# One decoder step of a 64-expert model on one core: the expert loop in 48 pairs of blocks instead of 96 single ones

## The reference

```python
scores = sigmoid(t @ w_r)                       # 264 x 64
idx = top 8 of 64, from the 4 best of 8 groups  # by scores + bias
gates = chosen scores / their sum * 2.5
for e in range(64):                             # 64 experts, 1024 -> 256 -> 1024
    a = silu(t @ wg[e]) * (t @ wu[e])
    routed += gates[:, e] * (a @ wd[e])
out = routed + shared expert
```

## Time and profile before

| what | value |
|---|---|
| runs, median (lowest to highest) | 1795.79 us (1793.62 to 1798.0) |
| the profiled execution | 1778.79 us, span 1777.1 us, granted clock 0.957 |
| PE busy | 1629.6 us, 92% |
| DVE busy | 957.6 us, 54% |
| POOL busy | 697.3 us, 39% |
| moved by DMA | 588.84 MB, mean 331 GB/s |

### The profile page before, as it was taken

How to read it: one execution, slowest core, us unless ns; L and a number is a source line. 1 busy time by engine, 2 the same in 40 slices (tenths; PEclk the granted TensorE clock), 3 DMA queues, 4 the chain that set the end, 5 groups by cost and what they waited for, 6 DMA issues and landing times.

```text
span 1777.1 us, 27285 instructions
## 1 busy us (share of the span) xinstructions
PE 1629.6 (92%) x10621; PEld 914.1 (51%) x10621; DVE 957.6 (54%) x2368; ACT 238.9 (13%) x607; POOL 697.3 (39%) x755
## 2 busy tenths in 40 slices
PE   7898999999899999999779989999998999899984
PEld 4674775444445444444367557644444444444433
DVE  3887468544345544444379754764443444354436
ACT  3223331000002100000031343100000000000001
POOL 1306007554445554444102240365554455355420
PEclk9998999999999999999979979999999999999996
DMA  9668467999999999999965866599999999999955
GB/s 326 226 237 289 154 266 277 400 364 357 401 408 400 385 413 393 377 382 360 346 239 190 287 216 235 189 395 412 410 389 409 346 387 405 367 386 399 413 209 207
DMA packets 185918, 588.84 MB, mean 331 GB/s; under 512 B 67705, under 2 KB 85837, under 8 KB 131902
## 3 DMA queue, kind: packets, MB, share of 16 engines
q1 hardware_dynamic: 115504, 506.99, 73.1%
q0 software_dynamic: 67232, 79.73, 13.0%
q10 hardware_dynamic: 3054, 0.38, 0.2%
HBM read 775.22 MB, written 56.95 MB: 468 GB/s over the span
## 4 chain that ended last, share of the span: by engine, by line
PE 80%; DVE 8%; DMA 5%; issue 3%; ACT 1%; ACTq 1%; SPq 0%; POOL 0%; DVEq 0%; POOLq 0%
PE ps L1420 39%; PE ps L1433 18%; PE ps L1122 4%; PE ps L953 4%; PE ps L1268 3%; DMA raw<-in_exp_w_up,idx_w 3%; PE ps L1009 2%; PE ps L1380 1%; DMA ypart<-yrows_k 1%; DVE ysum L2277 1%; PE ps L986 1%; PE ps L1017 1%; ACTq L577 1%; PE ps L1200 1%; PE ps L1253 1%
## 5 line engine op out<-in xcount | busy, mean ns | idle before, releaser
L1420 PE MATMUL ps<-raw,xTs 128*64 128x256 f32 x6144 | 744.0, 393 | 10.3 <-DMA raw<-in_exp_w_up,idx_w 7.0
L1420 PEld LDWEIGHTS ps<-raw,xTs 128*64 128x64 f32 x6144 | 417.2, 135 | 270.5 <-issue 11.7
L1433 PE MATMUL ps<-dn,scratch 128*64 128x512 f32 x1536 | 373.1, 607 | 38.9 <-issue 37.2
L900 POOL DMA_INDIRECT yrows_k<-ytok,idx_y x192 | 196.6, 1024 | 483.9 <-DVE ytok L2104 442.0
L2209 DVE STREAM_TRANSPOSE xTs<-xg 64x256 f32<-64x256 f32 x768 | 335.6, 437 | 8.8 <-DMA xg<-hrows,idx_x 1.0
L2104 DVE COPY ytok<-ps 128x512 f32<-128x512 f32 x192 | 132.8, 692 | 280.7 <-PE ps L1433 245.8
L893 POOL DMA_INDIRECT xg<-hrows,idx_x x192 | 199.1, 1037 | 105.9 <-DVE idx_x L2193 47.8
L2098 DVE TENSOR_TENSOR scratch<-scratch,ps 128x128 f32<-128x128 f32 x192 | 55.3, 288 | 316.2 <-ACT scratch L1718 316.0
L1433 PEld LDWEIGHTS ps<-dn,scratch 128*64 128x64 f32 x1536 | 109.3, 137 | 193.2 <-issue 163.6
L1718 ACT ACTIVATE scratch<-ps 128x128 f32<-128x128 f32 x192 | 53.2, 277 | 1108.7 <-PE ps L1420 1108.7
L1122 PE MATMUL ps<-hT,wide 128*128 128x264 f32 x512 | 121.6, 394 | 6.1 <-ACT hT L1539 6.1
(11 more groups left out here) (382 smaller groups left out, 1315.9 us busy)
## 6 DMA issues: line engine op xcount, KB each, us to landing
raw<-in_exp_w_gate SPq DMA_DIRECT2D x128, 1024.0 KB, 9.9
raw<-in_exp_w_up SPq DMA_DIRECT2D x128, 1024.0 KB, 14.9
dn<-in_exp_w_down SPq DMA_DIRECT2D x128, 1024.0 KB, 13.7
narrow<-in_w_ada SPq DMA_DIRECT2D x18, 1024.0 KB, 8.8
wide<-in_w_in SPq DMA_DIRECT2D x16, 1024.0 KB, 7.7
wide<-in_w_ada SPq DMA_DIRECT2D x16, 1024.0 KB, 8.9
ypart<-yrows_k SPq DMA_DIRECT2D x16, 1024.0 KB, 13.3
raw<-in_w_ada SPq DMA_DIRECT2D x14, 1024.0 KB, 12.7
```

What stands on the lines that cost most here:

```text
L900: pool.indirect_dma_start(yrows_k.rearrange("t (h d) -> (t h) d", h=2), bass.IndirectOffsetOnAxis(ap=idx_y[:, b:b + 1], axis=0), ytok[n % ...
L1420: ins = mm(ps[64 * h:64 * h + 64, 2 + n % 2, 0:256], xTs[n % 2][:, k, :, :].rearrange("p u i -> p (u i)"), w[:, k, h], start=k == 0, stop= ...
L1433: ins = mm(ps[64 * h:64 * h + 64, 5 + n % 2, :], actT[:, n % 2, 64 * j:64 * j + 64], dn[n % NDOWN][:, j, 512 * h:512 * h + 512], start=j = ...
```

## The change

The loop runs over 48 pairs of steps, m, each for steps 2m and 2m+1.

- `gate_up(m)`: tile 0 works on step 2m's tokens and weights, tile 1 on step 2m+1's. Each takes all 256 gate and 256 up columns, so 512 moving columns. It waits for both steps' weights and turned tokens.
- `down(m)`: tile 0 makes all 1024 output columns of step 2m's tokens in two halves, tile 1 those of step 2m+1. Two transposes stand between instead of one per step.
- ACT and DVE work on 256 columns (silu, act, actT, one buffer each) and 1024 (copy_y).
- `ytok` is two buffers of 1024 columns, and the scatter moves 128 rows of 4 KB per pair. Its row numbers, `idx_y`, are put together by eight small DVE operations instead of one.
- `xTs` has four buffers, and four steps are turned before the loop.
- Buffers of weights are released per pair: `raw` of steps 2m+5 and 2m+6 by gate_up(m), `dn` of steps 2m+4 and 2m+5 by down(m). The number of buffers and the order of SP's list are the same.
- `SPARE_AT` changes, so that the first four spare blocks stand on steps 14, 38, 62 and 86, as before, in another order.

```diff
-SPARE_AT = [(int(f"{s:05b}"[::-1], 2) + 4) % SPARE for s in range(SPARE)]
+SPARE_AT = [8 * (o % 4) + (o // 4 + 4) % 8 for o in range(SPARE)]
-NRAW, NDOWN, NX, NY = 5, 4, 8, 4
+NPAIR = NSTEP // 2
+NRAW, NDOWN, NX, NT, NY = 5, 4, 8, 4, 2
...
-                    sp.wait_ge(gu_made.sem, gu_made.by(layer, n - NRAW + 1))
+                    sp.wait_ge(gu_made.sem, gu_made.by(layer, (n - NRAW) // 2 + 1))
...
-                    sp.wait_ge(down_made.sem, down_made.by(layer, n - NDOWN + 1))
+                    sp.wait_ge(down_made.sem, down_made.by(layer, (n - NDOWN) // 2 + 1))
...
-            def scatter(n):
-                b = STEPS[n]
-                pool.wait_ge(y_copied.sem, y_copied.by(layer, n + 1))
-                pool.indirect_dma_start(yrows_k.rearrange("t (h d) -> (t h) d", h=2),
-                                        bass.IndirectOffsetOnAxis(ap=idx_y[:, b:b + 1], axis=0), ytok[n % NY][:, :], None,
-                                        bounds_check=2 * T * TOPK - 1, oob_is_err=False).then_inc(y_scattered[n % NY].sem, 16)
+            def scatter(m):
+                pool.wait_ge(y_copied.sem, y_copied.by(layer, m + 1))
+                pool.indirect_dma_start(yrows_k, bass.IndirectOffsetOnAxis(ap=idx_y[:, m:m + 1], axis=0), ytok[m % NY][:, :], None,
+                                        bounds_check=T * TOPK - 1, oob_is_err=False).then_inc(y_scattered[m % NY].sem, 16)
...
-            for n in range(NSTEP):
-                if n + NX < NSTEP:
-                    pool.wait_ge(x_turned.sem, x_turned.by(layer, n + 1))
-                    gather(n + NX)
-                m = n + NRAW
-                if m < NSTEP and STEPS[m] >= NE:
-                    pool.wait_ge(gu_made.sem, gu_made.by(layer, n + 1))
+            for m in range(NPAIR):
+                for n in (2 * m, 2 * m + 1):
+                    if n + NX < NSTEP:
+                        pool.wait_ge(x_turned.sem, x_turned.by(layer, n + 1))
+                        gather(n + NX)
+                for n in (2 * m + NRAW, 2 * m + NRAW + 1):
+                    if n < NSTEP and STEPS[n] >= NE:
+                        pool.wait_ge(gu_made.sem, gu_made.by(layer, m + 1))
...
-            def gate_up(n):
-                W(x_turned, n + 1)
-                pe.wait_ge(*raw_at_step(layer, n))
-                w = raw[n % NRAW][:, :, :].rearrange("p j (k q s) -> p k s j q", k=KD, s=2)
+            def gate_up(m):
+                W(x_turned, 2 * m + 2)
+                for n in (2 * m, 2 * m + 1):
+                    pe.wait_ge(*raw_at_step(layer, n))
                 for k in range(KD):
                     for h in range(2):
-                        ins = mm(ps[64 * h:64 * h + 64, 2 + n % 2, 0:256], xTs[n % 2][:, k, :, :].rearrange("p u i -> p (u i)"),
-                                 w[:, k, h], start=k == 0, stop=k == KD - 1, skip_group_check=True, tile_position=(0, 64 * h))
+                        n = 2 * m + h
+                        w = raw[n % NRAW][:, :, :].rearrange("p j (k n) -> p k j n", k=KD)
+                        ins = mm(ps[64 * h:64 * h + 64, 2 + m % 2, :], xTs[n % NT][:, k, :, :].rearrange("p u i -> p (u i)"),
+                                 w[:, k], start=k == 0, stop=k == KD - 1, skip_group_check=True, tile_position=(0, 64 * h))
                 ins.then_inc(gu_made.sem, 1)
...
+            def down(m):
+                W(actT_ready, m + 1)
+                for n in (2 * m, 2 * m + 1):
+                    pe.wait_ge(*down_at_step(layer, n))
+                if m >= 2:
+                    W(y_copied, m - 1)
...
+                for c in range(2):
+                    for j in range(2):
+                        for h in range(2):
+                            ins = mm(ps[64 * h:64 * h + 64, 5 * (m % 2) + c, :], actT[:, j, 64 * h:64 * h + 64],
+                                     dn[(2 * m + h) % NDOWN][:, j, 512 * c:512 * c + 512], start=j == 0, stop=j == 1,
+                                     skip_group_check=True, tile_position=(0, 64 * h))
...
-            for n in range(NSTEP):
-                gate_up(n)
-                if n >= 1:
-                    down(n - 1)
-                turn_act(n)
+            for m in range(NPAIR):
+                gate_up(m)
+                if m >= 1:
+                    down(m - 1)
+                turn_act(m)
```

More of the change, by code:

```diff
@@ L352, in program @@
     spare_is = scratch[:, PICK:PICK + SPARE * NE].rearrange("p (o e) -> p o e", o=SPARE)
-    silu, act, actT = (scratch[:, PICK + 256 * n:PICK + 256 * n + 256].rearrange("p (n f) -> p n f", n=2) for n in range(3))
+    silu = scratch[:, PICK:PICK + 256]
+    act, actT = (scratch[:, PICK + 256 * n:PICK + 256 * n + 256].rearrange("p (j f) -> p j f", j=2) for n in (1, 2))
     raw_at = [("vbuf", 0), ("kbuf", 0), ("wide", 0), ("projT", 0), ("wide", 2 * SEG)]
@@ L753, in _ @@
                 for q in range(ADA_FIRST):
-                    sp.wait_ge(gu_made.sem, gu_made.by(layer, STEP_OF_RAW[EARLY_RAW[q]] + 1))
+                    sp.wait_ge(gu_made.sem, gu_made.by(layer, STEP_OF_RAW[EARLY_RAW[q]] // 2 + 1))
                     early_ada(layer + 1, q)
@@ L944, in _ @@
-            scatter(NSTEP - 1)
+                if m >= 1:
+                    scatter(m - 1)
+                    for n in (2 * m - 2 + NDOWN, 2 * m - 1 + NDOWN):
+                        if n < NSTEP and STEPS[n] >= NE:
+                            spare_weights("exp_w_down", dn[n % NDOWN][:, :, :].rearrange("p j n -> p (j n)"), n, spare_down)
+            scatter(NPAIR - 1)
         pool.wait_ge(stores, DEPTH * layer_stores.per_layer)
@@ L1422, in gate_up @@
                 ins.then_inc(gu_made.sem, 1)
-            def down(n):
-                W(actT_ready, n + 1)
-                pe.wait_ge(*down_at_step(layer, n))
-                if n >= 2:
-                    W(y_copied, n - 1)
+            def down(m):
[4 more added lines that the diff above has]
+                    W(y_copied, m - 1)
                 else:
                     W(sh_copied, KD)
-                for j in range(2):
-                    for h in range(2):
-                        ins = mm(ps[64 * h:64 * h + 64, 5 + n % 2, :], actT[:, n % 2, 64 * j:64 * j + 64],
-                                 dn[n % NDOWN][:, j, 512 * h:512 * h + 512], start=j == 0, stop=j == 1,
-                                 skip_group_check=True, tile_position=(0, 64 * h))
-                ins.then_inc(down_made.sem, 1)
@@ L1448, in _, with turn_act @@
+                ins.then_inc(down_made.sem, 1)
+            def turn_act(m):
+                W(act_ready, m + 1)
+                for j in range(2):
+                    ins = turn(ps[:, 4, P * j:P * j + P], act[:, j, :], P)
+                ins.then_inc(act_turned.sem, 1)
+            for m in range(NPAIR):
+                gate_up(m)
+                if m >= 1:
+                    down(m - 1)
+                turn_act(m)
+                if m == PREP and layer + 1 < DEPTH:
                     turn_first(layer + 1)
-                if n == PREP_STEP + 3 and layer + 1 < DEPTH:
+                if m == PREP + 3 and layer + 1 < DEPTH:
@@ L1450, in _ @@
                     turn_mid(layer + 1, 7)
-                if n == PREP_STEP + 6 and layer + 1 < DEPTH:
+                if m == PREP + 6 and layer + 1 < DEPTH:
                     turn_late(layer + 1)
-            down(NSTEP - 1)
+            down(NPAIR - 1)
+            W(y_copied, NPAIR - 1)
             if layer + 1 < DEPTH:
@@ L1715, in _ @@
             W(spare_ready)
-            for n in range(NSTEP):
-                W(gu_made, n + 1)
-                act_(silu[:, n % 2, :], ps[:, 2 + n % 2, 0:128], ACT.Silu).then_inc(silu_ready.sem, 1)
-                if layer + 1 < DEPTH and n == PREP_STEP + 2:
+            for m in range(NPAIR):
+                W(gu_made, m + 1)
+                act_(silu, ps[:, 2 + m % 2, 0:256], ACT.Silu).then_inc(silu_ready.sem, 1)
+                if layer + 1 < DEPTH and m == PREP + 2:
                     prepare_exp(layer + 1)
-                elif layer + 1 < DEPTH and n == PREP_STEP + 4:
+                elif layer + 1 < DEPTH and m == PREP + 4:
                     prepare_more(layer + 1)
                     prepare_sin(layer + 1)
-                elif layer + 1 < DEPTH and n == PREP_STEP + 9:
+                elif layer + 1 < DEPTH and m == PREP + 9:
                     prepare_lam(layer + 1)
@@ L2194, in _ @@
             ins.then_inc(rows_ready.sem, 1)
-            ts(idx_y[:, :], table, 2.0, cst[:, K_Y:K_Y + 1], ALU.mult, ALU.add)
             chain(tt(spare_is, spare_upto.unsqueeze(1).to_broadcast([P, SPARE, NE]),
@@ L2234, in gates @@
                     chain(ins)
-            for n in range(2):
+            for n in range(NT):
                 turn_x(n)
-            for n in range(NSTEP):
-                activate(n)
-                if n >= 1:
-                    copy_y(n - 1)
-                copy_actT(n)
-                if n + 2 < NSTEP:
-                    turn_x(n + 2)
```

(10 more changed lines are left out.)

117 lines of the change are left out of this document (60 added, 57 removed).

## The result

| | median us (runs) | ratio to before, 95% interval |
|---|---|---|
| before | 1794.70 (8) | |
| after | 1808.67 (8) | 1.0082 [1.0065, 1.0100] |
| after, a second time (e10) | 1806.90 (6), before 1794.09 (23) | 1.0077 [1.0048, 1.0106] |

The change makes the kernel 0.8% slower, 13 to 14 us. The forecast was 1818, from a sum of +22. The profiled execution took 1811.23 us (span 1809.6), 32.4 more than before's 1778.79. That is not the change alone: before's profiled execution was 16 us faster than its own timed ones, after's was not. The experiments ran on three chips, and on these before's median was 1778.28, 1792.66 and 1794.09.

The account below looks back on a forecast made before the run. TensorE and DMA were both taken to be at their limit, DMA with less room (11.2 us against 11.50 per pair). Terms -13 + 10 + 16 + 4 + 5 = +22 gave 1801 profiled, 1818 by the runs' median; range 1775 to 1865.

Parts of the forecast that it names:

- TensorE's pair: Expert loop: a pair of steps takes TensorE 10.8 us against 11.50, 67 us over 96 if TensorE were alone.
- DMA decides in the loops: Expert loops: DMA needs 11.2 us per pair, so TensorE's faster 10.8 us pairs mostly wait for it.
- What DMA lets through: Expert loops: only time with DMA share below 1.02 for TensorE's sake can be taken; -13 us for both layers.
- the odd loads' lead: Odd steps' gate/up weights get 11.3 us of lead instead of 25; 0.3 us lost in three pairs, 32 times: +10.
- Start of the loop: Each layer's loop start: later buffer release delays weight loads, 8 of 10 us of DMA work lost for good; +16 for both.
- Used spares: Behind each used spare block one or two waits of 5 to 8 us; +0.6 for each of 7, +4.
- End: End of each loop: longer last down and copy delay scatter, final loads and next stage; +5 us for both.
- first rival: Expert loops: DMA stays full, odd loads nearly always land within 11.3 us; -16, 1780 us; chance 0.25.
- TensorE is not the bound: Judges the rival that TensorE bounds the loops and DMA follows to 10.8 us pairs: -62, 1734 us; chance 0.05.
- The halved clock: Rival: waits over 3 us, once per three pairs, make the next gate/up 1.6 us longer; 1869 us; chance 0.12.
- fourth rival: Gains and losses cancel: start +16, odd loads nothing, end +5, against -13 and -8 from software queue; 1796 us; chance 0.1.
- The rule weighed beside the sum: DMA engines alternate queues by packet; 640 instead of 768 rows per pair shrink software-queue lag by a sixth: -14, 1804 us.

Follow-up runs that it names:

- e10: The kernel after, unchanged, run again on the same chip as the kernel before: 1806.90 us, ratio 1.0077.
- e4: The kernel after with expert down loads from step 8 on cut to 256 of 2048 columns: 1687.00 us, ratio 0.9489.
- e3: The kernel before with expert down loads from step 8 on cut to 256 of 2048 columns: 1711.77 us, ratio 0.9619.
- e9: The kernel before, unchanged, profiled again on one chip with e10, e11 and e12: 1791.79 us (one run).
- e7: The kernel after with no spare block fetched, spares computing on what lies in the buffer: 1765.86 us, ratio 0.9844.
- e6: The kernel after with the next layer's w_ada loads moved ahead of the last two down loads, the fourth block last: 1812.67 us, ratio 1.0113.
- e12: e8 with blocks 1 to 3 of w_ada behind the last down load: 1793.04 us, ratio 0.9998.
- e2: The kernel before, single steps kept, with weight buffers released by pairs as in the kernel after: 1784.55 us, ratio 1.0042.
- e11: The kernel after with each down load one step later in SP's list from step 7 on, on e10's chip: 1792.92 us, ratio 0.9998.
- e5: The kernel after with eight idle matmuls ahead of the first gate/up of each layer: 1810.05 us, ratio 1.0098.
- e8: The kernel after with e1's order, e5's idle matmuls, e6's order, and scatter index writes behind the first two turned rows: 1796.82 us, ratio 1.0022.
- e1: The kernel after with each down load one step later in SP's list from step 7 on: 1790.39 us, ratio 1.0064.

## Why the prediction came out right

Size and sign were right: +14 for +22. Some of the steps were right, and errors of both signs cancelled, which was luck. By its own steps:

**TensorE's pair: right.** 10.82 us for 10.8, records 0.43 apart; e4 against e3 shows the gain once DMA has room (2.0 us in six free steps for 2.1).

**DMA decides in the loops: right.** Nearly the same bytes (446.2 and 441.6 MB) at the same share of 0.98 to 0.99; busy time per byte alike in e9 and e10. 22 MB less took 33 to 38 us off the loops (e7), and a cut of the down loads 66 us off the kernel before (e3).

**What DMA lets through, and the odd loads' lead (-13 and +10): right as a sum.** On one chip the calm stretches of six steps take 36.2 us before and 35.9 after, -7 for both layers; forecast -3. But 36.2 has e9's holds in it, so how much of the -7 is the change is open. The level was wrong: DMA's need was put at 3 x 11.2 = 33.6 us for six steps, and 35.9 were taken. They move 13.7 MB (four experts and a sixteenth of the rows), which at 0.392 MB per busy us is, as an estimate, 35 us of share, 8.7 for an expert where I had 8.6. The rest is that I divided by 1.02, the share of the best stretches, where calm ones reach 0.98 on average. The wait before every third pair was to be 2.7; in calm stretches it is 0.3 to 3.6, 2.0 on average, and the 2.91 above is one of the long ones. DMA's idle time in the middle of the loops is 29.8 for 22.7 us, but this includes the next two terms.

**Start of the loop (+16): right against the trace that was read, wrong for the chip of the timed runs.** I had gate/up(0) end at 283.8. Its records ended at 285.5, behind a gap of 3.7 us and at a lower clock (8.69 us for 7.09), and with the hold it was 288.0. So 21.1 us of DMA time were lost against the first trace (38.7 for 17.6), where 20 were forecast to be missing and 16 to count. But before's own start loses almost as much wherever it has the hold: idle 32.2 to 34.2 in e9 and e10. There the term is +2 by DMA's idle time, and by their own length the first six steps are even 14.4 us shorter after. Why the two differ so, no run separates.

**Used spares (+4): too small.** After, the seven six-step stretches in which a spare's fetch goes out cost 34.3 us above calm ones. Before, five stretches stand out, by 23.6 us: +11. One of these five, steps 48 to 53 of layer 0, holds no used spare but a wait of 2.49 us for VectorE; put with the calm ones it makes the term +14.5 and the calm one -10.5. Without the fetches (e7) the waits before pairs 6, 18 and 30 of layer 0 are 2.8, 3.3 and 4.8 us, with them (e10) 7.7, 8.4 and 8.3; that an odd main load with 11 us of lead is what they disturb is read from the list.

**A term that was missing, in layer 0.** Behind step 18's loads stands one small load whose issue takes SP about 9.5 us. SP in e10:

```profile
396.14 0.33 SPq L731 DMA_DIRECT2D dn<-in_exp_w_down  x1
...
397.00 9.55 SPq L578 DMA_DIRECT2D bst<-in_ssm_b_im  x1
406.60 4.50 SPq L716 DMA_DIRECT2D raw<-in_exp_w_gate  x1
```

TensorE then, also in e10:

```profile
429.72 4.54 PE L1423 MATMUL ps<-raw,xTs 128*64 128x512 f32 x10 [10.41 <-DMA raw<-in_exp_w_up]
```

Before it takes as long (9.51 in e9) and nobody waits: the lead covers it. These six steps take 44.1 us after and 36.4 before, +8 (in the first trace of before 40.8, with a wait of 3.40 us). The wait stays in e7, so it isn't the spares'; no run took the small load out. I had walked through the lead with weights alone and not asked what else stands in SP's list.

**Between the loops: missing too**, +11 in "between", with 4.2 MB less inside layer 0's loop. The w_ada loads go 18.5 us later (861.89 for 843.32) as they wait for gate/up by pairs and behind two down loads. In the DMA ledger it is the 4 us more of idle time in the last 40 us; e6 and e12 moved the loads and got no time from it, and in e2 the same shift stands at half the size (+5.3 with 2.2 MB less), so I put the rest down to the transfers and not the order.

**End (+5):** last rows of a loop 1.4 us longer, the tail 1.0 to 1.9, the first start 1.2 to 2.9 later: about right.

On one chip the sum, in rounded terms, is: calm stretches -7, first six steps -14, spares +11, parameters +8, last steps +2 (together -1 in the loops), between +11, start and tail +2: 11.9 between the profiled executions, 12.8 between the medians. So my +22 was near by luck: a start too dear against this chip (+16, where the first six steps have -14) made up for two terms that were missing and one too small.

The rivals. DMA was full, but the odd loads were not in time (first rival, half right). TensorE is not the bound. The halved clock is there: past the first two pairs of a loop in after and e10, no gate/up behind a wait of up to 1.9 us was slower, each behind 3.6 us or more was, by 1.3 to 3.0 us, and between them both occur. But the granted clock was 0.95 over the loops, not under 0.9. In e10 the slower gate/ups come to 32 us; in e11 slower gate/ups and downs come to 34, and it is 14 us faster. So the clock did not decide; that its cost falls where TensorE would wait for DMA anyway is how I read it. Of the fourth rival (1796) the cancelling is right and the terms are not: the odd loads do cost, and what cancels on this chip is in the loops alone (-1), not in the whole. The rule weighed beside the sum (1804) would have the software queue lag a sixth less. But its packets fall from 67232 before to 65696 after on the pages, 2.3%, and its share from 400 to 800 is 14.0% in e9 and 13.7% in e10, so nothing speaks for -14; the landings of after's scatters are not in the trace.

## What to carry to other kernels

Where DMA is the floor, work that TensorE saves buys nothing (e10 and e11, against e4). What counts is when each transfer may be issued, and for that read the issuing queue as one list: everything ahead of a load (a load waiting for a later event, a slow issue of 9.5 us) is part of its lead. A buffer's release by pairs is cheap (e2), a lead cut from 25 to 11 us is not, and one line's place in the list (e11) returned all 14 us, so that the kernel is as fast as before and no faster. Moving loads that are needed soon within a full stretch only moves the wait (e6, e12). When a profiled execution differs from the timed median by as much as the effect, profile both kernels on one chip before reading stages against each other.

## Unexpected of the hardware

- The hold of the first gate/up: in the first trace of after, in e5 to e8 and in e9 to e12 the engines that wait for it are released 1.8 to 3.8 us later than its last record implies, in both layers; in the first trace of before and in e1 to e4 (one chip) by 0.1 us. Between the chips before differs by 16 us. What holds TensorE no row shows: the profile names no instruction of this core as the releaser. No experiment was made on it.
- The same short wait is followed by a lower clock or not. Behind a wait of 2.91 us in after a gate/up took 8.78 us, behind one of 2.93 us in e10 it took 7.09. In e4 the first gate/ups stand behind 3.69 us in both layers and take 7.09 and 8.78.
- An order of issue that interleaves the same loads otherwise moved them at 0.393 and 0.397 MB per busy us (e11) instead of 0.390 and 0.394 (e10). e1, on another chip, has 0.393 and 0.397 too.
